# Attention without divided exponentials: inverse totals widened by GpSimd, turned by TensorE and multiplied into the outputs by VectorE

## The reference, cut to what matters

```python
s = q @ k.T * scale + mask          # 128 queries against up to 512 keys
p = exp(s - max(s)); p = p / sum(p) # softmax over the keys
o = p @ v                           # 64 wide for each head
```

## Time and profile before

| | us |
|---|---|
| median of 3 runs | 1748.63 |
| lowest and highest | 1746.57, 1749.33 |
| span of the profiled execution, first to last instruction | 1746.4 |
| attention stage in it, first score to the last remainder | 212.0 to 297.5 |
| PE busy over the whole span | 1692.4 (97%) |
| POOL busy over the whole span | 298.0 (17%) |

### The profile page before, as it was taken

One profiled execution on the slowest core, in us unless ns is written; L12 is line 12 of the kernel. 1 busy time (PEld: TensorE's weight loads), 2 busy tenths in 40 slices (PEclk: granted clock), 3 DMA queues, 4 the chain that ended last, 5 costly groups with the idle time before them and its releaser, 6 DMA issues.

```text
span 1746.4 us, 32411 instructions
## 1 busy us (share of the span) xinstructions
PE 1692.4 (97%) x12781; PEld 1504.0 (86%) x12781; DVE 1093.3 (63%) x1748; ACT 744.9 (43%) x1111; POOL 298.0 (17%) x286
## 2 busy tenths in 40 slices
PE   5999999999999999899999999999999999999998
PEld 4776666788888888799999999999999999989986
DVE  6766576777764668855858664344753766754633
ACT  4467575454332342532323545346323643322323
POOL 2112196210000002432005221110102000000002
PEclk8999999999999999999999999999999999999999
DMA  9453532443333232264335752332543233332332
GB/s 310 124 141 102 157 110 84 135 97 107 99 95 98 84 108 67 85 172 124 127 105 152 224 141 87 99 117 80 166 117 96 74 94 91 92 97 85 96 95 75
DMA packets 321167, 201.18 MB, mean 115 GB/s; under 512 B 51279, under 2 KB 303814, under 8 KB 320918
## 3 DMA queue, kind: packets, MB, share of 16 engines
q1 hardware_dynamic: 300976, 160.79, 32.4%
q0 software_dynamic: 7952, 24.83, 4.7%
q10 hardware_dynamic: 12118, 13.88, 2.3%
HBM read 177.75 MB, written 17.24 MB: 112 GB/s over the span
## 4 chain that ended last, share of the span: by engine, by line
PE 84%; DVE 6%; ACT 4%; SPq 2%; issue 2%; DMA 1%; POOL 1%; ACTq 0%; DVEq 0%; POOLq 0%
PE ps L1467 69%; SPq L854 2%; PE ps L1608 1%; DVE wlo L2175 1%; PE ps L1769 1%; PE ps L1667 1%; PE ps L1779 1%; PE ps L1795 1%; PE ps L2020 1%; PE ps L1682 1%; PE ps L1584 1%; ACT whi L912 1%; DMA xrow<-in_x_dram 1%; PE ps L1946 0%; PE ps L1536 0%
## 5 line engine op out<-in xcount | busy, mean ns | idle before, releaser
L1467 PE MATMUL ps<-zhi,whi 128*128 128x258 f32 (+2 forms) x2072 | 639.2, 308 | 1.4 <-ACT ub L1201 0.6
L1467 PE MATMUL ps<-zlo,whi 128*128 128x258 f32 (+2 forms) x2072 | 633.4, 306 | 0.0
L1467 PE MATMUL ps<-zhi,wlo 128*128 128x258 f32 (+2 forms) x2072 | 632.1, 305 | 0.0
L1467 PEld LDWEIGHTS ps<-zhi,whi 128*128 128x128 f32 x2072 | 390.8, 189 | 25.5 <-issue 2.2
L2175 DVE TENSOR_TENSOR wlo<-stage,whi 128x1024 fp32r<-128x1024 f32 x256 | 324.9, 1270 | 136.0 <-ACT whi L912 124.0
L1467 PEld LDWEIGHTS ps<-zlo,whi 128*128 128x128 f32 x2072 | 390.2, 188 | 19.7 <-issue 1.2
L1467 PEld LDWEIGHTS ps<-zhi,wlo 128*128 128x128 f32 x2072 | 390.9, 189 | 18.0
L912 ACT ACTIVATE whi<-stage 128x1024 fp32r<-128x1024 f32 x256 | 269.4, 1055 | 305.2 <-PE ps L1467 253.7
L1467 PE MATMUL ps<-ghi,whi 128*128 128x512 f32 x340 | 134.7, 396 | 0.0
L1467 PE MATMUL ps<-glo,whi 128*128 128x512 f32 x340 | 134.2, 395 | 0.0
L1467 PE MATMUL ps<-ghi,wlo 128*128 128x512 f32 x340 | 134.0, 394 | 0.0
(11 more groups left out here) (432 smaller groups left out, 2833.5 us busy)
## 6 DMA issues: line engine op xcount, KB each, us to landing
stage<-in_w_up_dram SPq DMA_DIRECT2D x88, 512.0 KB, 3.8
stage<-in_w_in_dram SPq DMA_DIRECT2D x74, 512.0 KB, 4.0
stage<-in_w_down_dram SPq DMA_DIRECT2D x32, 512.0 KB, 4.0
ring<-in_w_ada_dram POOLq DMA_DIRECT2D x24, 512.0 KB, 4.4
adab<-in_w_ada_dram SPq DMA_DIRECT2D x16, 512.0 KB, 7.8
stage<-in_w_down_dram SPq DMA_DIRECT2D x16, 384.0 KB, 3.4
stage<-in_w_o_dram SPq DMA_DIRECT2D x8, 512.0 KB, 4.1
ring<-in_w_ada_dram SPq DMA_DIRECT2D x8, 512.0 KB, 3.7
```

The costliest lines, as they stand in the source:

```text
L1467: last = pe.matmul(out, w(a, k), x(k, t0, t1), start=(k == 0 and a is whi and x is x_hi), stop=(k == ks - 1 and a is wlo))
```

## The change: what it does

The exponentials are no longer divided. PE turns them as ACT leaves them, as soon as `at_exp` says so, and `values` makes undivided outputs, which lie with the head's 64 columns across the partitions and the queries along the free axis. The division is done once for a group of four steps, on the 128x512 outputs:

- DVE writes the reciprocals of eight steps in turn to 16 columns (`inverses`).
- POOL copies the eight columns of a group to `invwide`, 128x512, each repeated 64 times, raises `inv_wide`, and then takes the remainder `mlo` of the group before.
- PE transposes `invwide` in four blocks into the bank of PSUM that the group's outputs don't use (`inverse_rows`, in iteration t % 4 == 2, from t = 6), which makes rows of inverses in the layout of the outputs.
- ACT copies that bank to `rowinv` (in the place where `mhi` was, t % 4 == 3). The next group's v0 writes the same bank of PSUM, so it waits for `inv_done`.
- DVE multiplies the outputs by `rowinv` into `mix` (in the place of `mlo`, t % 4 == 0 from t = 8), and ACT rounds `mix` to `mhi` in that same iteration.
- The last group's `mlo` is taken by DVE, behind its `mhi`.

```diff
@@ -284,6 +284,8 @@
         diag = at("diag", [P, QB, P], TAB + 14336)
         asum = {g: at(f"asum{g}", [P, D], b) for g, b in ((2, TAB + 8192), (3, ZUO + 8192), (4, TAB + 8192), (5, TAB + 12288))}
         rtp = at("rtp", [P, 2, T1], TAB + 8192 + 4096)
+        mix = at("mix", [P, 2, T1], TAB + 8192 + 4096)
+        rowinv, invwide = at("rowinv", [P, T1], ZUO + 8192), at("invwide", [P, QB, P], ZUO + 10240)
         ring = [[at(f"ring{n}{i}", [P, D], b + 4096 * i) for i in range(RING)] for n, b in enumerate((FREE + 16384, ZUO))]
         wide_ring = ring[1] + [at(f"ring1{2 + i}", [P, D], TAB + 4096 * i) for i in range(2)]
 
@@ -422,7 +424,9 @@
         gln_done = sem("gln_done")
         at_s, at_mask, at_exp, at_t, at_o = sem("at_s"), sem("at_mask"), sem("at_exp"), sem("at_t"), sem("at_o")
         at_pt = [sem("at_pt0"), sem("at_pt1")]
-        at_rec, at_p = sem("at_rec"), sem("at_p")
+        at_rec, inv_mm = sem("at_rec"), sem("inv_mm")
+        inv_done, mix_done, INV0 = xt_done, xt_mm, KD
+        inv_wide, WIDE0 = tab_ready, 2
         mixhi, mixlo = sem("mixhi"), sem("mixlo")
         mod_read = sem("mod_read")
         conv_done, silu_done, gf_done, ghi_done, glo_done = (sem("conv_done"), sem("silu_done"), sem("gf_done"),
@@ -607,9 +611,14 @@
         def least(t, r):
             return small[:, 8 + 2 * (t % 4) + r:9 + 2 * (t % 4) + r]
 
-        def total(t, r, base=16):
-            c = base + 2 * (t % 4) + r
+        def total(t, r):
+            c = 16 + 2 * (t % 4) + r
             return small[:, c:c + 1]
+
+        def inverses(t, n=1):
+
+            c = 32 + 2 * (t % 8)
+            return small[:, c:c + 2 * n]
 
         FFNS = [dict(T=T1, up="w_up", down="w_down", cw="cw", cb="cb", key="b1", g2=40),
                 dict(T=T3, up="w_up_2", down="w_down_2", cw="cw2", cb="cb2", key="b2", g2=None)]
@@ -1149,8 +1158,12 @@
                     split_hi(U["wo"] + WO_HI.index(t))
                 if t >= 7 and t % QB == 3:
                     m = (t - 7) // QB
-                    act.wait_ge(at_o, QB * m + QB)
-                    act.activation(mhi[:, (m + 4) % 8, :], ps[:, 6 + m % 2, :], ACT.Copy).then_inc(mixhi, 1)
+                    act.wait_ge(inv_mm, m + 1)
+                    act.activation(rowinv[:, :], ps[:, 7 - m % 2, :], ACT.Copy).then_inc(inv_done, 1)
+                if t >= 8 and t % QB == 0:
+                    m = (t - 8) // QB
+                    act.wait_ge(mix_done, INV0 + m + 1)
+                    act.activation(mhi[:, (m + 4) % 8, :], mix[:, m % 2, :], ACT.Copy).then_inc(mixhi, 1)
             for j in range(8):
                 split_hi(U["wo"] + 3 + j)
                 if 1 <= j < 7:
@@ -1772,7 +1785,7 @@
 
                 i = STEPS[q][2]
                 for r in range(2):
-                    pe.wait_ge(at_p, 2 * q + r + 1)
+                    pe.wait_ge(at_exp, 2 * q + r + 1)
                     if q:
                         pe.wait_ge(at_pt[r], q)
                     for j in range(i + 1):
@@ -1787,14 +1800,23 @@
                 m = q // QB
                 for r in range(2):
                     pe.wait_ge(at_pt[r], q + 1)
-                if i == 0 and m >= 2:
-                    pe.wait_ge(mixlo, m - 1)
+                if i == 0 and m:
+                    pe.wait_ge(inv_done, INV0 + m)
                 for j in range(i + 1):
                     for r in range(2):
                         h = 2 * hp + r
                         mm = pe.matmul(ps[HD * r:HD * r + HD, 6 + m % 2, i * P:(i + 1) * P], V[:, j, h * HD:(h + 1) * HD],
                                        PT[:, q % 2, r, j * P:(j + 1) * P], start=j == 0, stop=j == i)
                 mm.then_inc(at_o, 1)
+
+            def inverse_rows(m):
+
+                pe.wait_ge(inv_wide, WIDE0 + m + 1)
+                if m:
+                    pe.wait_ge(mix_done, INV0 + m)
+                for i in range(QB):
+                    mm = pe.transpose(ps[:, 7 - m % 2, i * P:(i + 1) * P], invwide[:, i, :], const("ident"))
+                mm.then_inc(inv_mm, 1)
 
             pe.wait_ge(ghead_done, 5)
             wait_job_out(pe, J["dv"] + 2)
@@ -1828,6 +1850,8 @@
                     values(t - 4)
                 if 3 <= t < NS + 3:
                     turn(t - 3)
+                if t >= 6 and t % QB == 2:
+                    inverse_rows((t - 6) // QB)
 
 
             wo_first(KD - 1, KD)
@@ -2473,10 +2497,9 @@
                 if 1 <= t <= NS:
                     q = t - 1
                     dve.wait_ge(at_exp, 2 * q + 2)
-                    if q >= 4:
-                        dve.wait_ge(at_p, 2 * (q - 4) + 2)
-                    dve.reciprocal(small[:, 32 + 2 * (q % 4):34 + 2 * (q % 4)], small[:, 16 + 2 * (q % 4):18 + 2 * (q % 4)])\
-                       .then_inc(at_rec, 1)
+                    if q >= 2 * QB:
+                        dve.wait_ge(inv_wide, WIDE0 + q // QB - 1)
+                    dve.reciprocal(inverses(q), small[:, 16 + 2 * (q % 4):18 + 2 * (q % 4)]).then_inc(at_rec, 1)
                 if 3 <= t < NS + 3:
                     q = t - 3
                     w = (STEPS[q][2] + 1) * P
@@ -2488,9 +2511,16 @@
                     split_lo(U["wo"] + WO_LO.index(t))
                 if t >= 8 and t % QB == 0:
                     m = (t - 8) // QB
-                    dve.wait_ge(mixhi, m + 1)
-                    dve.tensor_tensor(mlo[:, (m + 4) % 8, :], ps[:, 6 + m % 2, :], mhi[:, (m + 4) % 8, :].bitcast(F32), ALU.subtract)\
-                       .then_inc(mixlo, 1)
+                    dve.wait_ge(at_o, QB * m + QB)
+                    dve.wait_ge(inv_done, INV0 + m + 1)
+                    if m >= 2:
+                        dve.wait_ge(mixlo, m - 1)
+                    dve.tensor_tensor(mix[:, m % 2, :], ps[:, 6 + m % 2, :], rowinv[:, :], ALU.mult).then_inc(mix_done, 1)
+
+            dve.wait_ge(mixlo, HEADS - 1)
+            dve.wait_ge(mixhi, HEADS)
+            dve.tensor_tensor(mlo[:, 3, :], mix[:, 1, :], mhi[:, 3, :].bitcast(F32), ALU.subtract).then_inc(mixlo, 1)
+            dve.wait_ge(mixlo, HEADS)
 
             def residual(job, T, gate, m, i, base):
 
@@ -3044,12 +3074,18 @@
             for a in range(24, 34):
                 ada_load(pool, a)
 
-            for t in range(NS):
-                w = (STEPS[t][2] + 1) * P
-                pool.wait_ge(at_rec, t + 1)
-                for r in range(2):
-                    pool.tensor_scalar(pb[:, t % 4, r, 0:w], pb[:, t % 4, r, 0:w], total(t, r, 32), None, ALU.mult)\
-                        .then_inc(at_p, 1)
+            for m in range(HEADS):
+                pool.wait_ge(at_rec, QB * m + QB)
+                if m:
+                    pool.wait_ge(inv_mm, m)
+                pool.tensor_copy(invwide[:, :, :].rearrange("p i (r d) -> p (i r) d", r=2),
+                                 inverses(QB * m, QB).unsqueeze(2).to_broadcast([P, 2 * QB, HD])).then_inc(inv_wide, 1)
+                if m:
+                    k = (m + 3) % 8
+                    pool.wait_ge(mixhi, m)
+                    pool.tensor_tensor(mlo[:, k, :], mix[:, (m - 1) % 2, :], mhi[:, k, :].bitcast(F32), ALU.subtract)\
+                        .then_inc(mixlo, 1)
+
             def add_square(n, j):
 
                 pool.wait_ge(sq_done, SQ0[n] + j + 1)
```

## The result

The changed kernel takes 1763.85 us in the median of 5 runs (1761.39 to 1765.66), the kernel before 1748.63 beside it. The ratio is 1.0086, interval 1.0074 to 1.0098: slower by 13 to 17 us. The forecast was 1758.6, the range 1753.5 to 1764.0. The profiled execution's span is 1759.6, 13.2 above the one before.

A forecast was written before the change was run, and what follows sets the result against it. PE was taken to bound the stage, with GpSimd in its shadow. Terms 1.8 + 2.5 + 0.5 + 4.2 + 0.1 + 0.2 + 0.7 = 10.0 us on the 1746.4 span, plus 2.2 to the median, gave 1758.6; range 1753.5 to 1764.0.

The forecast's parts named there:

- What bounds the kernel: In the stage, PE bounds and GpSimd lies in its shadow; removing GpSimd's multiplications returns 0.7 us, all in the first period.
- v0's wait for `rowinv`: On PE, v0 waits for ACT's copy and comes 0.95 us later; with the transposes, each mla period grows 1.40 us.
- The transposes: Four added on PE per group, with the wait ahead of them 0.45 us on the path, bounds 0.44 and 0.60.
- The `dil` periods: The first three periods grow by 1.8, 2.5 and 0.5 us, to 11.2, 12.25 and 10.3.
- The soft term of the second: In the second dil period, ACT's mhi waits for DVE's mix behind wlo: +1.0 us, bounds 0 and 1.2.
- The clock: Rival: PE idles before the second and third v0 and at the end lower its clock; 1762 to 1764 us, 14 in 100.
- the prediction's own signs of being wrong: In the stage: mla periods under 10.5 us, PE waiting for POOL, or a granted clock under 1.00.
- The end: At the stage's end mix stands ahead of mhi, mlo and the product, and PE waits for all three: +0.7 us.
- the drain: In the drain one set of transposes lies mostly beside a copy on DVE: +0.2 us.
- The widening on GpSimd: A 128x512 copy a group on GpSimd, costed at nothing; bounds 0.6 and 4 us, hidden at both.
- the 25 named as a sign: Sign of the forecast holding: GpSimd's share of the stage falls to some 25 us.

The follow-up runs named there:

- with the clock kept up: Changed kernel plus matmuls of constants in PE's idle time, ahead of the second and third dil v0 and at the stage's end; 1757.38 us, ratio 1.0053.
- the early copy: Changed kernel, but ACT copies to rowinv at its iteration's start, ahead of the exponential of head 0 of s3; 1751.99 us, ratio 1.0026.
- the splits moved: Changed kernel with ACT's three splits of weights at t = 5, 6 and 10 instead of 6, 7 and 11; 1760.68 us, ratio 1.0065.

## Why the prediction was right, and where it was off

*What bounds the kernel.* Right. GpSimd lay in PE's shadow, and taking it away gave 0.7 us in the first period, the figure taken. The figure itself was chosen from between 0 and 3.0 without a sum behind it, so that it hit is partly luck.

*v0's wait for `rowinv`.* Right in place, order and size. From t0 to v0 1.87 us were worked out; in the changed kernel's `mla` half it is 262.26 to 264.23, 1.97. The periods grew by 1.47 to 1.49 for a forecast of 1.40. Moving the copy up took the waits away.

*The transposes.* Forecast 0.45 a group on the path; doubling them added 0.44 to an `mla` period.

*The `dil` periods.* Forecast 11.2, 12.25 and 10.3; with the clock kept up they are 11.29, 12.22 and 10.34. The soft term of the second, the wait of ACT for a `mix` that stands behind `wlo`, is there: ACT waits 1.85 us for DVE's `mix`. That period agrees with it, but no run took the term out by itself.

*The clock.* This is the step that was off: the sum put it at nothing and gave the case 14 in 100. It came, three times, and cost 0.55, 1.47 and 1.5 us, together 3.5. The terms that the sum does have come to 10.5 with the clock kept up, where 10.0 were forecast; 10.5 and 3.5, less the 0.9 elsewhere, are the 13.2 of the spans (each rounded). So the measured median is the one that the rival named, 1762 to 1764, and not the 1758.6 of the forecast. It stands in the range only because the upper end was drawn for that rival, and only 0.15 us below it; two of the five executions lie above. And a granted clock under 1.00 in the stage was among the prediction's own signs of being wrong. That the range held is the rival's merit and some luck, while the waits and their sizes were worked out. The argument against it was the weak point: that 1.05 us of idle had left the clock alone says nothing of 2.2, and the prediction itself had a row with 2.08 of idle and a fall behind it. It should have had the larger chance. That the Trainium skill (TensorE: Matmul & The Clock Gate, Part 4: PE-mode transpose) says that transposes don't count as busy in the same way is not needed for the falls: the early copy issues just as many transposes, and its clock stays at 1.00 until it idles 2.25 us at the end.

*The end.* Forecast 0.7 for the end and 0.2 for the drain, measured 1.05 together.

*The widening on GpSimd.* Costed at nothing, and nothing waited for it. The copy is done at 227.46, and PE comes to the transposes at 235.25. GpSimd's work in the stage is 13.8 us, not the 25 named as a sign: both of its instructions turned out shorter than the 1.80 us taken from the earlier trace rows.

## What to carry to other kernels

An engine busy in nine tenths of a stage can still be worth nothing: ask how many steps lie between its input and its consumer, and test it by leaving its work out before replacing it. When a short instruction on a shared engine starts to gate the engine that bounds, its place in the queue is worth more than its length; here one 0.58 us copy, moved ahead of an exponential into time the engine spent waiting, was worth about 10.5 us, the clock's share included. And price a new idle of the matmul engine twice, once as time and once as the clock that may fall behind it.

## What the runs showed of the hardware

- The granted clock of TensorE went from 2.4 to 1.2 GHz behind idles of 2.20 and 2.25 us: three of three in the changed kernel, one of one in the early copy, one of one with the splits moved, two of three with the transposes doubled (its first, 2.20 us, left the clock at 1.00). In the attention stage it never fell behind 1.74, 1.26, 1.23 and 1.09. A fall in the `dil` half cost 0.55 and 1.47 us, the one at the end 1.5, where PE has no other waits.
- The length of the longest single idle doesn't decide it alone. The kernel before has no wait of PE over 1.6 us behind 320 us, and yet its clock falls there. One of these falls stands behind two shorter waits close together. First PE's timeline, then its busy time and clock from 1356 to 1358 us:

```profile
1353.24 0.67 PE L1561 MATMUL ps<-sq,cst 128*128 128x258 f32 x2 [1.26 <-ACT sq L929]
1354.78 0.50 PE L1584 MATMUL ps<-zhi,whi 128*128 128x258 f32 x1 [0.87 <-DVE zlo L2204]
```

```profile
1356.00:1358.00 2.00, 2.00 (x11) 2.00 (x11) 1.62 (x6) 1.97 (x6) 0.00 (x0) 0.50 0.00 0
```

- GpSimd's widening copy to 128x512 takes 0.61 us, and its remainder of two 128x512 tiles 1.27, where its multiplication of a tile had a mean of 1.15 over all widths and its addition 1.80. All 8 copies lie within 4 ns.

```profile
L3081 POOL COPY invwide<-small x8: 609/610/613, 217.8 to 298.3; 128x512 f32<-128x512 f32 x8
...
```

```profile
L3086 POOL TENSOR_TENSOR mlo<-mix,mhi x7: 1266/1270/1277, 232.5 to 301.5; 128x512 fp32r<-128x512 f32 x7
...
```

- GpSimd held DVE up. In the early copy DVE's `wlo`, 1.22 us in the median, takes 1.97 beside GpSimd's remainder, which takes its usual 1.27:

```profile
229.47 1.27 POOL L3086 TENSOR_TENSOR mlo<-mix,mhi 128x512 fp32r<-128x512 f32 x1 [2.47 <-ACT mhi L1166]
...
229.85 1.97 DVE L2199 TENSOR_TENSOR wlo<-stage,whi 128x1024 fp32r<-128x1024 f32 x1
```

The Trainium skill (SBUF — State Buffer, SBUF: two separate sides) has the two engines take turns at a shared pair of ports when DVE reads two tensors of SBUF. The trace fits nearly: GpSimd ends at 230.74, DVE's 1.22 counted from there ends at 231.96, and it ended at 231.82, 0.14 sooner. DVE had slack there: before its next 512-wide mask it waited 0.29 us for PE's scores. So the period shows no loss.
